# The gathers of the next expert's tokens moved from steps 11 to 14 of an expert to steps 9 to 12

## The chip, the cores and the metric

The kernel runs on one core of a Trainium2 chip. A core has a matrix engine (TensorE, PE in the profile; PEld are its weight loads, which overlap its products), a vector engine (VectorE, DVE), a scalar engine (ScalarE, ACT), GpSimd (POOL) and a queue engine (SyncE, SP) that here issues the loads of weights from HBM. The metric is the device time in microseconds (us) of one execution; lower is better.

## The reference

Two two-layer blocks run one after the other on 256 tokens of width 1024, all in float32. The change touches one part of the first block, the mixture of experts in its second layer:

```
def moe_swiglu(h, w_router, w_gate, w_up, w_down):
    logits = jnp.einsum('bsd,de->bse', h, w_router).astype(jnp.float32)
    top_v, top_i = lax.top_k(logits, TOP_K)
    wts = jax.nn.softmax(top_v, axis=-1)
    gates = jnp.sum(jax.nn.one_hot(top_i, N_EXPERTS, dtype=jnp.float32) * wts[..., None], axis=-2)
    ...
        a = jnp.einsum('sd,edf->sef', hb, w_gate)
        u = jnp.einsum('sd,edf->sef', hb, w_up)
        act = jax.nn.silu(a) * u * gb[:, :, None]
        return jnp.einsum('sef,efd->sd', act, w_down)
```

## The kernel before, in words

**Tiling.** Each expert computes only the tokens routed to it, at most 128 of them in one pass; a second pass exists in the code and is jumped over when no expert has more. The 3584 hidden columns of an expert are cut into 14 steps of 256 (`MOE_STEPS`), so the stage has 8 x 14 = 112 steps. A step loads 3 MiB of weights (1 MiB each for the two halves of gate and up, and one for down) into a ring of 6 slots, `ring`.

**Rounding to two terms.** Every float32 weight is used as a high and a low part. ACT writes the high part of a slot to another buffer (L637), DVE leaves the low part in the slot (L645), and `product` (L136 to L138) makes three matrix products of each pair of operands. PE can begin with a slot only after DVE's L645 on it.

**A step on each engine.** PE: `gate_up` (24 products of 512 columns), `down` of the step before (12 products), `turn` (two transposes, L2311). ACT: silu of the step (L2448), three high parts (L637), and a copy of the transposes (L2454). DVE: the product with silu's output (L2509), the low part of the transposes (L2513), three low parts (L645). SP waits until PE has finished `gate_up` or `down` on a slot, and then issues the next load into it, in the fixed order gate and up, gate and up, down (`moe_pass_sp`).

**The gather.** The tokens of the next expert are picked by products with a one-hot matrix: `gather(e1, g, ...)` in PE (L2290), for two of the eight chunks of 128 features, g = 0 to 3. Of each round ACT makes the high part (L2432) and DVE the low part (L2497, L2501); DVE's L2501 raises the semaphore `hTb`. Four such rounds fill `hTe`/`hLe` of the other half, a double buffer that alternates between experts. `gather` stands between `down` and `turn` of its step. Each round but the first waits for `hTb` of the round before, since all use the same piece of PSUM (`later_gather`). Ahead of the first product of the next expert, PE waits for the last `hTb`:

```
        pe.wait_ge(E['hTb'], e * 4 + (8 + moe_before(p, 'hTb')))
        gate_up(1 - half, 0, m1)
        down(1, m0 + (MOE_STEPS - 1), False, True)
        turn(m1)
        gate_up(1 - half, 1, m0 + (MOE_STEPS + 1))
        scatter(e)
```

The scatter (L2330) adds the finished expert's rows to the sum, in the second step of the next expert.

**Loops.** The program is written out by hand. An outer loop (L2240) runs three times over a pair of experts; experts 7 and 8 are written out behind it. In an expert an inner loop (L2336 in PE, L2252 in ACT and DVE) runs over pairs of steps up to `GATHER_STEP`, and the steps from there on are written out one by one, with the gathers. The first two steps of the next expert are written out as well. In the names of the trace `rT` is the one-hot matrix, `z_rounded` the high part of the gathered tokens, and `AT`, `AT_rounded` in one half and `ada`, `ada_rounded` in the other are the low part. Transposes of step n are called turn n here, counted from 1 to 14 in each expert.

Of the kernel before, what the change touches and what calls it, by code (L numbers as in the profile page):

```python
# [132 lines left out]
def product(pe, out, a, b, start, stop):  # L133


    pe.matmul(out, r32(a[0]), r32(b[1]), start=start, stop=False, skip_group_check=True)  # L136
    pe.matmul(out, r32(a[1]), r32(b[0]), start=False, stop=False, skip_group_check=True)  # L137
    return pe.matmul(out, r32(a[0]), r32(b[0]), start=False, stop=stop, skip_group_check=True)  # L138
# [18 lines left out]
def chunks(ap, k, w):  # L157

    return ap[:, 0:k * w].rearrange('p (k w) -> p k w', k=k)
# [469 lines left out]
def ffn_slot(st, q, r):  # L629
    return (st['j0'] + 3 * r + q) % RING  # L630
# [1495 lines left out]
MOE_STEPS = F_EXPERT // FT  # L2126
# [24 lines left out]
def moe_sems(c, p):  # L2151

    E = {name: c.s[name if p == 0 else f'again_{name}'] for name in ('gu_hi', 'gu_lo', 'down_hi', 'down_lo')}
    return E | {name: c.s[f'me_{name}'] for name in MOE_COUNTS}


def moe_before(p, name):
    return p * MOE_COUNTS[name]
# [72 lines left out]
def moe_split_value(st, q, m, p):  # L2231
    return split_value(st if p == 0 else dict(split0=0), q, m)


GATHER_STEP = MOE_STEPS - 4


def moe_experts(eng, expert):

    with eng.Fori(0, (N_EXP - 2) // 2) as pair:  # L2240
        for half in range(2):
            expert(pair * 2 + half, pair * (2 * MOE_STEPS) + half * MOE_STEPS, half, None)
    for e in (N_EXP - 2, N_EXP - 1):
        expert(e, e * MOE_STEPS, e % 2, e)


def moe_body_loop(eng, body, extra, next_extra, end):


    def expert(e, m0, half, known):  # L2250
        last = known == N_EXP - 1
        with eng.Fori(1, GATHER_STEP // 2) as it:  # L2252
            for r in range(2):
                body(r, m0 + it * 2 + r, 2, None)
        for i in range(GATHER_STEP, MOE_STEPS):
            ahead = min(2, MOE_STEPS - 1 - i) if last else 2
            body(i % 2, m0 + i, ahead, None if last else (lambda i=i: extra(e, half, i - GATHER_STEP)))
        if last:
            end(e)
            return  # L2260
        body(0, m0 + MOE_STEPS, 2, lambda: next_extra(e, known))
        body(1, m0 + (MOE_STEPS + 1), 2, None)
    for r in range(2):
        body(r, r, 2, None)
    moe_experts(eng, expert)


def first_gather(c, g):

    return c.pb[4 + g][:, 0:S]  # L2270


def later_gather(c):
    return c.pb[7][:, S:2 * S]


def moe_pass_pe(c, pe, st, p):
    E = moe_sems(c, p)
    G, T = c.pb[6], c.pb[7]

    def gather(e1, g, out, before):

        if g == 0:
            pe.wait_ge(E['onehot'], e1 + moe_before(p, 'onehot'))
        elif before is not None:
            pe.wait_ge(E['hTb'], before)
        for i in range(2):
            kc = 2 * g + i
            for n in range(NT):
                mm = pe.matmul(out[:, i * P:i * P + P], c.xn[:, n, kc * P:kc * P + P], c.onehot[:, n, :],  # L2290
                               start=n == 0, stop=n == NT - 1)
        mm.then_inc(E['gathered'], 1)

    def parts(q, r, n):
        slot = ffn_slot(st, q, r)
        return chunks(c.hi_moe[slot], n, SLOT // n), chunks(c.ring[:, slot, :], n, SLOT // n)

    def gate_up(half, r, m):
        hTe, hLe = c.hTe[half], c.hLe[half]
        for q in range(2):  # L2300
            pe.wait_ge(E['gu_lo'], moe_split_value(st, q, m, p))
            wh, wl = parts(q, r, 4)
            for i in range(4):
                x = 4 * q + i
                mm = product(pe, G[:, :], (hTe[:, x, :], hLe[:, x, :]), (wh[:, i, :], wl[:, i, :]), x == 0, x == KD - 1)
        mm.then_inc(E['gu'], 1)

    def turn(m):
        pe.wait_ge(E['act'], m + (1 + moe_before(p, 'act')))
        for a in range(2):  # L2310
            mm = pe.transpose(T[:, a * P:a * P + P], c.fa[:, 0, a * P:a * P + P], c.ident[:, :])  # L2311
        mm.then_inc(E['turned'], 1)

    def down(r, m, first, last):
        pe.wait_ge(E['down_lo'], moe_split_value(st, 2, m, p))
        pe.wait_ge(E['actT'], m + (1 + moe_before(p, 'actT')))
        wh, wl = parts(2, r, 2)
        for h in range(2):
            col = slice(h * 512, h * 512 + 512)
            for a in range(2):  # L2320
                mm = product(pe, c.pb[4 + h][:, :], (c.faT[:, 0, a, :], c.faL[:, 0, a, :]), (wh[:, a, col], wl[:, a, col]),
                             first and a == 0, last and a == 1)
        mm.then_inc(E['down'], 1)

    def scatter(e):
        pe.wait_ge(E['ye'], e + (1 + moe_before(p, 'ye')))
        pe.wait_ge(E['sums'], e + (1 + moe_before(p, 'sums')))
        for n in range(NT):
            for h in range(2):
                mm = pe.matmul(c.pb[2 * n + h][:, :], c.combine[:, n * P:n * P + P], c.ye[:, h * 512:h * 512 + 512],  # L2330
                               start=False, stop=False, skip_group_check=True)
        mm.then_inc(E['scat'], 1)

    def expert(e, m0, half, known):
        last = known == N_EXP - 1
        with pe.Fori(1, GATHER_STEP // 2) as it:  # L2336
            for r in range(2):
                m = m0 + it * 2 + r
                gate_up(half, r, m)
                down(1 - r, m - 1, False, False)  # L2340
                turn(m)
        for i in range(GATHER_STEP, MOE_STEPS):
            g = i - GATHER_STEP
            gate_up(half, i % 2, m0 + i)
            down(1 - i % 2, m0 + (i - 1), False, False)
            if not last:
                gather(e + 2, g, later_gather(c), e * 4 + (4 + g + moe_before(p, 'hTb')))
            turn(m0 + i)
        if last:
            down(1, m0 + (MOE_STEPS - 1), False, True)  # L2350
            scatter(e)
            return

        m1 = m0 + MOE_STEPS
# [6 lines that stand above are left out]
        down(0, m1, True, False)  # L2361
        turn(m0 + (MOE_STEPS + 1))
    for g in range(4):
        gather(1, g, first_gather(c, g), None)
    pe.wait_ge(E['hTb'], 4 + moe_before(p, 'hTb'))
    gate_up(0, 0, 0)
    turn(0)
    gate_up(0, 1, 1)
    down(0, 0, True, False)
    turn(1)  # L2370
    moe_experts(pe, expert)


# [577 lines left out]
```

## Time and profile before

| | us |
|---|---|
| median of 3 runs | 2813.42 (2812.7 to 2815.88) |
| the profiled execution | 2820.07 |
| its span, from the first to the last instruction | 2817.7 |
| PE busy | 2357.3 (84% of the span) |
| DVE busy | 1868.7 (66%) |
| ACT busy | 1333.8 (47%) |
| steps of the expert stage, first turn to last turn | 811.5 to 1854.4 |
| mean granted TensorE clock | 0.898 of full speed |

Shares are averages over stages with different limits; the expert stage takes about 1050 us of the span. A step of that stage is measured here from turn to turn, the starts of two L2311 rows of PE.

### The profile page before, as it was taken

How to read it: one execution, taken by the hardware profiler on the slowest of the kernel's cores; microseconds unless marked ns; L12 is line 12 of the kernel's file. 1: busy time of each engine (PE TensorE's matmuls, PEld its weight loads, DVE VectorE, ACT ScalarE, POOL GpSimd, SP SyncE). 2: the span in 40 equal slices, each digit the busy share in tenths (PEclk: the TensorE clock that was granted, in tenths of full speed). 3: DMA queues.
4: the chain of work that ended last, by engine and by line, in shares of the span. 5: the costliest groups of instructions: out<-in, count | busy, mean ns of one | idle time of the engine just before them, and what ended most of it. 6: DMA issues, size and time to landing. Idle time of an engine off the chain costs nothing.

```text
span 2817.7 us, 30853 instructions
## 1 busy us (share of the span) xinstructions
PE 2357.3 (84%) x11193; PEld 1935.7 (69%) x11193; DVE 1868.7 (66%) x1975; ACT 1333.8 (47%) x1416; POOL 42.2 (1%) x102
## 2 busy tenths in 40 slices
PE   4836899855689999999999999966869987476998
PEld 4726687744567787777777777846758876465786
DVE  7776766776468787878888887855444443544553
ACT  3412433522247676766776676742334443232542
POOL 1000000000000000000000000000000000000000
PEclk9856999976689999999999999977979998688999
DMA  8730687530159899999999998953315552131453
GB/s 304 259 108 15 212 294 279 189 105 0 45 172 357 304 354 314 353 314 336 334 334 340 323 344 306 359 201 120 124 44 181 191 176 87 60 105 59 136 179 127
DMA packets 412832, 594.81 MB, mean 211 GB/s; under 512 B 20315, under 2 KB 326726, under 8 KB 412742
## 3 DMA queue, kind: packets, MB, share of 16 engines
q1 hardware_dynamic: 407040, 586.55, 60.4%
q10 hardware_dynamic: 5702, 7.04, 0.7%
q8 instruction: 58, 0.95, 0.1%
q14 instruction: 32, 0.26, 0.0%
HBM read 592.47 MB, written 1.05 MB: 211 GB/s over the span
## 4 chain that ended last, share of the span: by engine, by line
PE 72%; DVE 13%; ACT 5%; issue 3%; DMA 3%; POOL 1%; SPq 0%; ACTq 0%; DVEq 0%; POOLq 0%
PE bank L136 21%; PE bank L138 20%; PE bank L137 20%; DMA ring<-in_moe_w_up 2%; DVE ring_rounded L645 1%; PE bank L2330 1%; PE bank L1135 1%; PE bank L1113 1%; DVE ring_rounded L287 1%; ACT L L1187 1%; PE bank L2290 1%; PE bank L2311 1%; PE bank L1651 1%; PE bank L1124 1%; PE bank L461 1%
## 5 line engine op out<-in xcount | busy, mean ns | idle before, releaser
L136 PE MATMUL bank<-ring_rounded,hT_rounded 128*128 128x512 f32 (+3 forms) x944 | 376.9, 399 | 50.2 <-DVE ring_rounded L287 47.4
L136 PE MATMUL bank<-ring_rounded,z_rounded 128*128 128x512 f32 x896 | 365.9, 408 | 24.9 <-DVE AT_rounded L2501 11.4
L645 DVE TENSOR_TENSOR ring_rounded<-ring,zT_rounded 128x2048 fp32r<-128x2048 f32 x147 | 336.9, 2292 | 62.9 <-ACT zT_rounded L637 61.1
L136 PE MATMUL bank<-ring_rounded,L_rounded 128*128 128x512 f32 x712 | 290.5, 408 | 15.8 <-DVE score_rounded L778 10.5
L637 ACT ACTIVATE zT_rounded<-ring 128x2048 fp32r<-128x2048 f32 x147 | 281.6, 1916 | 31.6 <-DMA ring<-in_moe_w_up 16.6
L136 PEld LDWEIGHTS bank<-ring_rounded,hT_rounded 128*128 128x128 f32 x944 | 183.0, 194 | 88.3 <-issue 54.4
L136 PEld LDWEIGHTS bank<-ring_rounded,z_rounded 128*128 128x128 f32 x896 | 170.6, 190 | 67.6 <-issue 21.5
L645 DVE TENSOR_TENSOR ring_rounded<-ring,PT_rounded 128x2048 fp32r<-128x2048 f32 x74 | 169.4, 2289 | 39.9 <-ACT PT_rounded L637 39.5
L645 DVE TENSOR_TENSOR ring_rounded<-ring,mix_rounded 128x2048 fp32r<-128x2048 f32 x71 | 162.5, 2288 | 29.3 <-ACT mix_rounded L637 29.0
L136 PEld LDWEIGHTS bank<-ring_rounded,L_rounded 128*128 128x128 f32 x712 | 134.3, 189 | 56.2 <-DVE ring_rounded L645 19.4
L637 ACT ACTIVATE PT_rounded<-ring 128x2048 fp32r<-128x2048 f32 x74 | 141.7, 1915 | 37.9 <-DMA ring<-in_moe_w_up 36.4
L637 ACT ACTIVATE mix_rounded<-ring 128x2048 fp32r<-128x2048 f32 x71 | 136.2, 1919 | 29.0 <-DMA ring<-in_moe_w_up 27.9
L645 DVE TENSOR_TENSOR ring_rounded<-ring,hT_rounded 128x2048 fp32r<-128x2048 f32 x56 | 128.3, 2291 | 27.1 <-ACT hT_rounded L637 27.1
L138 PE MATMUL bank<-zT_rounded,L_rounded 128*128 128x512 f32 x368 | 146.1, 397 | 0.0
L137 PE MATMUL bank<-zT_rounded,score_rounded 128*128 128x512 f32 x368 | 144.6, 393 | 0.0
L645 DVE TENSOR_TENSOR ring_rounded<-ring,hL_rounded 128x2048 fp32r<-128x2048 f32 x56 | 128.3, 2291 | 13.4 <-ACT hL_rounded L637 12.8
L745 ACT ACTIVATE L_rounded<-bank 128x256 fp32r<-128x256 f32 x66 | 25.3, 383 | 220.6 <-PE bank L696 220.5
L778 DVE TENSOR_TENSOR score_rounded<-bank,L_rounded 128x256 fp32r<-128x256 f32 x66 | 27.8, 421 | 146.1 <-ACT L_rounded L745 146.0
L137 PE MATMUL bank<-hT_rounded,ring_rounded 128*128 128x256 f32 x416 | 120.4, 290 | 0.0
L637 ACT ACTIVATE hT_rounded<-ring 128x2048 fp32r<-128x2048 f32 x56 | 107.3, 1916 | 24.4 <-DMA ring<-in_moe_w_up 24.1
L137 PE MATMUL bank<-PT_rounded,hL_rounded 128*128 128x512 f32 (+2 forms) x282 | 112.7, 400 | 0.0
L278 ACT ACTIVATE PT_rounded<-ring 128x2048 fp32r<-128x2048 f32 (+3 forms) x31 | 53.3, 1719 | 123.2 <-DVEq L2850 40.5
(464 smaller groups left out, 5547.4 us busy)
## 6 DMA issues: line engine op xcount, KB each, us to landing
ring<-in_moe_w_gate SPq DMA_DIRECT2D x224, 512.0 KB, 5.3
ring<-in_moe_w_up SPq DMA_DIRECT2D x224, 512.0 KB, 6.8
ring<-in_moe_w_down SPq DMA_DIRECT2D x224, 512.0 KB, 7.8
ring<-in_ffn_w_gate_up SPq DMA_DIRECT2D x88, 512.0 KB, 5.1
ring<-in_ffn_w_down SPq DMA_DIRECT2D x66, 512.0 KB, 7.9
ring<-in_w_ada SPq DMA_DIRECT2D x48, 512.0 KB, 7.1
ring<-in_w_in SPq DMA_DIRECT2D x32, 512.0 KB, 4.9
xn<-in_w_ada SPq DMA_DIRECT2D x24, 512.0 KB, 9.6
```

The lines of the kernel that those rows point to most:

```text
L136: pe.matmul(out, r32(a[0]), r32(b[1]), start=start, stop=False, skip_group_check=True)
L137: pe.matmul(out, r32(a[1]), r32(b[0]), start=False, stop=False, skip_group_check=True)
L138: return pe.matmul(out, r32(a[0]), r32(b[0]), start=False, stop=stop, skip_group_check=True)
L278: act.activation(r32(st['hi'][(s - st['s0']) % H][:, 0:n]), c.ring[:, j % RING, 0:n], ACT.Copy)\
L287: dve.tensor_tensor(r32(words), words, high(st['hi'][(s - st['s0']) % len(st['hi'])][:, 0:n]), ALU.subtract)\
L461: mm = pe.transpose(c.pb[j][:, i * S + n * P:i * S + n * P + P], c.xn[:, n, kc * P:kc * P + P], c.ident[:, :])
L637: act.activation(r32(hi[slot]), c.ring[:, slot, :], ACT.Copy).then_inc(sem, 1)
L645: dve.tensor_tensor(r32(w), w, high(hi[slot]), ALU.subtract).then_inc(sem_out, 1)
L1113: mm = pe.matmul(c.pb[bank][:, u * S:u * S + s], a['q'](i, n), a['k'](i, n), start=True, stop=True)
L1124: mm = pe.transpose(c.pb[4 + b % 3][:, (blk % 4) * P:(blk % 4) * P + P], c.L[:, i * S + ch * P:i * S + ch * P + P], c.ident[:, :])
L1135: mm = pe.matmul(out, v, c.PT[:, blk * P:(blk + m) * P], start=x == 0, stop=x == len(terms) - 1)
L1187: act.activation(row, row, ACT.Exp, bias=c.nmx[:, i:i + 1], scale=a['scale'], accum_out=c.esum[:, i:i + 1]).then_inc(c.s['att_exp'], 1)
```

## The change

The four gathers stand in steps 9 to 12 of an expert (its last two steps have none), where they stood in steps 11 to 14. For that, the inner loop ends two steps earlier, and six steps are written out in place of four.

```
-GATHER_STEP = MOE_STEPS - 4
+GATHER_STEP = MOE_STEPS - 6
+GATHERS = 4
...
         for i in range(GATHER_STEP, MOE_STEPS):
             ahead = min(2, MOE_STEPS - 1 - i) if last else 2
-            body(i % 2, m0 + i, ahead, None if last else (lambda i=i: extra(e, half, i - GATHER_STEP)))
+            g = i - GATHER_STEP
+            body(i % 2, m0 + i, ahead, None if last or g >= GATHERS else (lambda g=g: extra(e, half, g)))
...
             gate_up(half, i % 2, m0 + i)
             down(1 - i % 2, m0 + (i - 1), False, False)
-            if not last:
+            if not last and g < GATHERS:
                 gather(e + 2, g, later_gather(c), e * 4 + (4 + g + moe_before(p, 'hTb')))
             turn(m0 + i)
```

Line numbers below the changed places are higher by 2 in the new kernel (L2311 is L2313 there).

PE before, end of the first expert of a pair (last products of `down`, last gather, turn 14, then the wait and the next expert's first `gate_up`):

```order
L137 MATMUL bank<-hL_rounded,score_rounded 128x512
L138 MATMUL bank<-hL_rounded,L_rounded 128x512
L2286 REGISTER_ALU
L2290 MATMUL bank<-rT,xn 128x128 x4
L2309 REGISTER_ALU
L2311 MATMUL bank<-ident,L 128x128 x2
L2355 REGISTER_ALU
L2301 ISA
L136 MATMUL bank<-ring_rounded,z_rounded 128x512
```

PE in the changed kernel, the same place:

```order
L137 MATMUL bank<-hL_rounded,score_rounded 128x512
L138 MATMUL bank<-hL_rounded,L_rounded 128x512
L2311 REGISTER_ALU
L2313 MATMUL bank<-ident,L 128x128 x2
L2357 REGISTER_ALU
L2303 ISA
L136 MATMUL bank<-ring_rounded,z_rounded 128x512
```

The gather's four products are gone from here; two whole steps now lie between the last of them and this place.

DVE before, step 14 of the first expert of a pair (low part of a slot, of the transposes, of the gathered tokens, then two slots):

```order
L645 TENSOR_TENSOR ring_rounded<-ring,hT_rounded 128x2048
L2513 TENSOR_TENSOR score_rounded<-bank,L_rounded 128x256
L2493 REGISTER_ALU
L2497 TENSOR_SCALAR ada<-bank,modA,modC 128x128 x2
L2501 TENSOR_TENSOR ada_rounded<-ada,z_rounded 128x256
L643 REGISTER_ALU
L645 TENSOR_TENSOR ring_rounded<-ring,zT_rounded 128x2048
L643 ISA
L645 TENSOR_TENSOR ring_rounded<-ring,PT_rounded 128x2048
```

DVE in the changed kernel, step 14:

```order
L645 TENSOR_TENSOR ring_rounded<-ring,hT_rounded 128x2048
L2515 TENSOR_TENSOR score_rounded<-bank,L_rounded 128x256
L643 REGISTER_ALU
L645 TENSOR_TENSOR ring_rounded<-ring,zT_rounded 128x2048
L643 ISA
L645 TENSOR_TENSOR ring_rounded<-ring,PT_rounded 128x2048
```

The three operations of the gather left step 14 (and step 13) and stand in the same place of steps 9 and 10.

## Rows read from the trace of the kernel before

**Rows 1.** The page: span, busy time, and 40 slices of the span.

```profile
span 2817.7 us, 30853 instructions
...
PE   4836899855689999999999999966869987476998
...
PEclk9856999976689999999999999977979998688999
DMA  8730687530159899999999998953315552131453
```

**Rows 2.** Waits of PE and SP, 929 to 1739 us: total, times, longest.

```profile
PE bank L136 <- DVE ada_rounded L2501: 11.4, 4, 2.9
PE bank L136 <- DVE AT_rounded L2501: 8.6, 3, 2.9
...
PE bank L136 <- DVE ring_rounded L645: 1.1, 2, 0.6
...
PEld bank L136 <- DVE ring_rounded L645: 8.5, 25, 1.0
```

**Rows 3.** Timeline from a turn 14 to the next expert's products: start, us, engine.

```profile
1195.41 0.38 PE L2311 MATMUL bank<-ident,L 128*128 128x128 f32 x2
...
1195.91 0.81 ACT L2432 ACTIVATE z_rounded<-bank,modC,modA 128x128 fp32r<-128x128 f32 x2 [1.96 <-PE bank L2311]
...
1197.03 0.42 DVE L2513 TENSOR_TENSOR score_rounded<-bank,L_rounded 128x256 fp32r<-128x256 f32 x1 [0.72 <-ACT L_rounded L2454]
1197.37 0.72 DVE L2497 TENSOR_SCALAR ada<-bank,modA,modC 128x128 f32<-128x128 f32 x2
1198.12 0.42 DVE L2501 TENSOR_TENSOR ada_rounded<-ada,z_rounded 128x256 fp32r<-128x256 f32 x1
...
1198.68 0.49 PE L136 MATMUL bank<-ring_rounded,z_rounded 128*128 128x512 f32 x1 [2.88 <-DVE ada_rounded L2501]
1199.01 0.40 PE L137 MATMUL bank<-mix_rounded,ada_rounded 128*128 128x512 f32 x1
...
1201.10 0.63 PE L137 MATMUL bank<-mix_rounded,ada_rounded 128*128 128x512 f32 x1
```

**Rows 4.** Windows, turn 14 to turn 1: us, engines' busy time, PEclk, DMA share, GB/s.

```profile
1195.41:1208.68 13.27, 10.39 (x41) 8.11 (x40) 7.67 (x9) 6.87 (x7) 0.00 (x0) 0.87 0.61 207
...
1460.18:1471.92 11.74, 8.86 (x40) 6.96 (x39) 7.94 (x9) 6.87 (x7) 0.00 (x0) 1.00 0.68 235
...
sum 91.15, PE 71.13 PEld 55.60 DVE 54.50 ACT 48.07 POOL 0.00; mean PE 10.16 PEld 7.94 DVE 7.79 ACT 6.87 POOL 0.00
```

**Rows 5.** Windows, turn 2 to turn 10 of seven experts, eight steps each.

```profile
1353.75:1422.05 68.30, 68.30 (x306) 55.47 (x305) 57.89 (x39) 51.01 (x40) 0.00 (x0) 1.00 1.01 349
...
sum 486.90, PE 483.65 PEld 386.35 DVE 407.91 ACT 358.42 POOL 0.00; mean PE 69.09 PEld 55.19 DVE 58.27 ACT 51.20 POOL 0.00
```

**Rows 6.** Windows, turn 10 to turn 14 of seven experts, four steps each.

```profile
1290.26:1328.57 38.31, 38.31 (x185) 31.27 (x185) 34.57 (x30) 27.30 (x27) 0.00 (x0) 1.00 0.99 339
...
sum 267.88, PE 267.26 PEld 218.86 DVE 240.88 ACT 191.37 POOL 0.00; mean PE 38.18 PEld 31.27 DVE 34.41 ACT 27.34 POOL 0.00
```

**Rows 7.** Window, turn 1 to turn 2, with the scatter.

```profile
1605.21:1617.12 11.91, 11.91 (x47) 8.45 (x46) 9.80 (x9) 7.26 (x7) 0.00 (x0) 1.00 1.04 358
```

**Rows 8.** DMA queues in the first pass of the outer loop, 829 to 1095 us.

```profile
q8 instruction: 6, 0.10, 0.2%
```

**Rows 9.** DMA queues from 1100 to 1600 us: all packets, and the one queue.

```profile
DMA packets 128130, 168.42 MB, mean 337 GB/s; under 512 B 5149, under 2 KB 114306, under 8 KB 128130
...
q1 hardware_dynamic: 128130, 168.42, 97.5%
```

**Rows 10.** Branches of PE's sequencer, and PE behind the second: ns min/median/max, starts.

```profile
L2240 PEldq COMPARE_BRANCH  x3: 67/209/217, 1084.9 to 1613.9; - x3
...
L2215 PEldq COMPARE_BRANCH  x1: 4832/4832/4832, 1866.9 to 1866.9; - x1
...
1871.81 1.10 PE L2420 MATMUL bank<-zero 128*128 128x256 f32 x2 [2.07 <-issue]
```

## The prediction

> **What bounds the kernel now.** I read the page's slices first. From about slice 12 to slice 27, the expert stage, PE is at nine tenths or more and its clock is full but for a dip here and there; the DMA engines are as busy [rows 1]. So two resources are near their limit there, and the question is which one PE waits for. The waits of PE over six experts answer it: there is one large entry, DVE's L2501, in seven waits of 2.9 us each, 11.4 + 8.6 = 20.0 us in all; on weights (DVE's L645) PE itself waits 1.1 us in total, and its weight loads 8.5 us in 25 small pieces [rows 2]. L2501 is the last low part of the gathered tokens, and seven is the number of passages from one expert to the next.
>
> The timeline of one passage shows the chain [rows 3]. Turn 14 starts at 1195.41. ACT can take the last gather only when turn 14 is done (L2432 at 1195.91, released by L2311), because its gather stands behind its wait for the turn; DVE follows with L2513, L2497 and L2501, which ends at 1198.54; PE starts the next expert's first product at 1198.68. PE's own idle time is 2.88 us. Behind it the record of a product grows from 0.40 us to 0.63, so the passage costs more than the idle time.
>
> The windows price it whole. From turn 14 to turn 1 of the next expert takes 13.27 us with a mean granted clock of 0.87; in one passage of the seven the clock stayed at 1.00, and it took 11.74 [rows 4]. Thus the drop of the clock from its upper level (2.4 GHz) to its lower (1.2 GHz) for a few us behind the idle stretch is worth 1.5 us, six times. The seven passages together are 91.15 us [rows 4]. A step with neither gather nor scatter, averaged over 56 of them, takes 486.90 / 56 = 8.69 us, and in the best expert 68.30 / 8 = 8.54 [rows 5]. A step with a gather takes 267.88 / 28 = 9.57 us, with PE busy in 267.26 of the 267.88 us [rows 6]: the gather there is PE's own work, 0.88 us more. The step with the scatter takes about 11.9 us [rows 7].
>
> **The change part by part.**
>
> *The gathers on PE.* The same four rounds, 0.88 us each, move from the steps that end in turns 11 to 14 to those that end in turns 9 to 12. Removed and added work cancel: 0. No wait is added. The first round needs the one-hot matrix, written by DVE in the first step of the same expert, eight steps earlier; each further round needs L2501 of the round before, as now, with a step between them. The buffer that they fill was last read by the expert before. No DMA is issued by them. SP waits for the ends of `gate_up` and `down`, whose order is unchanged.
>
> *ACT and DVE.* They get the same operations two steps earlier. In a step with a gather DVE is busy 240.88 / 28 = 8.60 us of 9.57 [rows 6], in one without it 407.91 / 56 = 7.28 of 8.69 [rows 5]. Both fit, and the new steps 13 and 14 are of the second kind.
>
> *The wait for `hTb`.* It is satisfied two steps, some 17 us, before PE comes to it. The passage then is a step like any other: `gate_up`, `down`, turn. What is late next is a slot of weights, since the first `gate_up` of the next expert needs L645 on its slots. In the timeline of now that low part was made a step ahead, as in all other steps, so I take the average plain step, which has such waits in it. 91.15 - 7 x 8.69 = 91.15 - 60.8 = **30.3 us** gained, of which 20.0 is idle time and the rest mostly the clock. With the plain step of the best expert it would be 91.15 - 7 x 8.54 = 31.4.
>
> *The loads.* Where I charge nothing for them, the cover is this. A step loads 3 x 1.049 = 3.146 MB. The stall now gives the DMA a rest: 207 GB/s in that window [rows 4]. Without it an expert takes 9 x 8.69 + 4 x 9.57 + 11.9 = 128.4 us for 44.0 MB, 343 GB/s on average; the windows show 349 over eight steps and 358 in the step of the scatter, when the queue catches up [rows 5, 7]. At 358 GB/s a step's load takes 8.79 us: 0.78 less than a step with a gather and 0.1 more than a plain one. The four gather steps let the loads run up to the limit of the ring, and the three plain steps that now lie between them and the scatter (steps 13, 14 and the next expert's first) give back 0.3. The scatter's 3.3 us then refill the ring, as now, so what follows it starts from the same state. Up to 1 us per passage may still be lost, the longest single wait for weights [rows 2]; this goes into the range.
>
> *The code.* Six steps are written out in place of four, in each half of the outer loop's body. By the counts of the windows a step is 76 instructions on PE (305 products and as many weight loads in eight steps) [rows 5], a gather 16 more and the scatter about as many [rows 6, 7]: the body grows from 16 x 76 + 8 x 16 + 2 x 16 = 1376 to 20 x 76 + 160 = 1680. In its first pass PE's instruction queue fetched 6 blocks [rows 8]; in the 500 us after 1100, with two returns to the start of the body in sight of it, none at all: the only queue with packets is that of the loads [rows 9]. So the chip keeps the present body, and whether it keeps one of 1680 / 1376 x 6 = 7.3 blocks no row shows. Bounds: nothing, if it does; if it does not, a jump to code that is not there is the 4.83 us branch at L2215, behind which PE was idle 2.07 us [rows 10]. The jump back at L2240 is taken with a lead: the sequencer is there at 1613.9, turn 2 begins at 1617.12 [rows 7, 10], 3.2 us later. That leaves 4.8 - 3.2 = 1.6 us per jump, two jumps, 3.2 us. I take nothing, as the nearest row shows no fetch [rows 9], and keep 3.2 for the range.
>
> The Trainium skill, Runtime: NRT & Kernel Launch, section Instruction fetch mechanics, speaks against the change here: it gives PE a store of 128 KiB, 2048 instructions in blocks of 16 KiB, eight of them, and says that a taken branch whose target is outside a window of two blocks forces a fetch. By its two-block window the present kernel would fetch at each return, which the trace contradicts; by its 2048 instructions the new body, which would touch eight blocks and call for a ninth, is just at the limit. That page would give 3.2 us less gain, the row as it stands gives none.
>
> **The sum.** 30.3 us off the profiled execution's 2820.07 is 2789.8. That execution is 6.65 us over the median of the runs, 2813.42; carried over, 2783.1.
>
> **The rivals.**
>
> 1. *Refetch at the return.* The body no longer fits by one block: 2 x 1.6 = 3.2 us, 2786. For it: it grows by a fifth. Against: nothing in the trace but the lead of the sequencer, which hides most of it.
>
> 2. *Weights take the stall's place.* PE now comes to the next expert 4.3 us earlier each time, and the loads were almost continuous before. If the three plain steps ahead of the scatter each waited 0.5 us, half the longest wait seen, it is 7 x 3 x 0.5 = 10.5, so 2794. For it: DMA share 1.01 to 1.04 in the windows [rows 5, 7]. Against: PE lost only 486.90 - 483.65 = 3.3 us to idle time in 56 plain steps.
>
> 3. *DMA is the true bound.* If the loads could not do more than the 337 GB/s seen between 1100 and 1600 us [rows 9], an expert needs 130.7 us; now it takes 8 x 8.69 + 4 x 9.57 + 13.02 + 11.9 = 132.7, so 2.0 x 7 = 14 us, 2799; at the 332 that the present pace amounts to (44.0 MB in 132.7 us), nothing, 2813. Against: the 358 above.
>
> 4. *Slower: the code streams through.* If the store works so that a body one block too long misses in every block, two passes of eight blocks at up to 4.83 us are 77 us, of which sequential fetching hides some. It decides from 30.3 / 16 = 1.9 us exposed per block on; fully exposed it is 2783 + 77 = 2860. Against: in the first pass, where each block was new as well, PE showed no other waits than in the later ones [rows 2].
>
> **How the numbers follow.** A measurement of this kernel can tell about 0.2%, 5.6 us, from no change. Forecast 0.60; rival 1 0.15; rival 2 0.14; rival 3 0.06 (half of it within 0.2%); rival 4 0.03, and 0.02 that the passages stay as they are for a reason I don't see. Faster: 0.60 + 0.15 + 0.14 + 0.03 = 0.92. Same: 0.03 + 0.02 = 0.05. Slower: 0.03. The range reaches from 2779 (the best expert's plain step, 2782, less the spread of the runs, 3 us) to 2796 (rival 2 and the spread).
>
> **What would show it.** No wait of PE for L2501 at the seven passages; turn 14 to turn 1 at 8.5 to 8.8 us with a clock of 1.00; turn 8 to turn 12 at 9.57 a step; the DMA rate over the stage from 332 to 343 GB/s. Rival 1 shows as blocks on the instruction queue during the second and third pass and a gap behind L2240's successor; rival 2 as waits for L645 in steps 13 to 1. The forecast is wrong if those waits exceed 1 us a passage, or if a clock below 1.00 remains in the stage.

## The result and the profile after

| | before | changed |
|---|---|---|
| median of 13 runs, us | 2818.26 | 2799.32 |
| profiled execution, us | 2820.07 | 2796.46 |
| its span, us | 2817.7 | 2794.7 |

The ratio of the times is 0.9939, with a 95% interval of 0.9925 to 0.9954: 0.61% faster, 17 us, where 1.08% (30.3 us) was forecast. One run of 5986.56 us, more than twice the others, is left out of the ratio.

The waits of PE from 905 to 1730 us in the changed kernel (total, times, longest), to be held against [rows 2]:

```profile
PE bank L136 <- issue: 6.7, 2, 3.5
PE bank L136 <- DVE ring_rounded L645: 1.4, 2, 1.1
PE bank L2313 <- DVE L L2511: 0.5, 2, 0.3
```

The seven waits for the gathered tokens, 20.0 us, are gone. In their place stand two waits of 3.3 and 3.5 us that the profile ascribes to "issue": PE waited for nothing it shows. The windows of the passages, turn 14 to turn 1 (us, busy time of each engine, clock, DMA share, GB/s), answer to [rows 4]:

```profile
927.70:936.34 8.64, 8.64 (x39) 6.97 (x39) 7.48 (x5) 6.64 (x6) 0.00 (x0) 1.00 1.05 362
...
1316.59:1325.08 8.49, 8.49 (x40) 6.93 (x38) 7.24 (x5) 5.80 (x5) 0.00 (x0) 1.00 1.04 361
...
1704.93:1715.23 10.30, 9.01 (x40) 6.69 (x38) 7.54 (x5) 7.99 (x6) 0.00 (x0) 1.00 0.99 337
sum 62.69, PE 61.16 PEld 47.69 DVE 52.43 ACT 47.31 POOL 0.00; mean PE 8.74 PEld 6.81 DVE 7.49 ACT 6.76 POOL 0.00
```

91.15 us became 62.69, a gain of 28.5, and the clock stays at 1.00 in every one. The four steps with a gather, now turn 8 to turn 12, cost what they did in [rows 6]:

```profile
sum 266.71, PE 266.71 PEld 218.87 DVE 240.08 ACT 191.58 POOL 0.00; mean PE 38.10 PEld 31.27 DVE 34.30 ACT 27.37 POOL 0.00
```

What was given back stands at turn 2 to turn 3 of experts 3 and 5, right behind the outer loop's return; the same steps of the kernel before took 8.49 and 8.48 us by the same reading of its turns:

```profile
1076.65:1090.30 13.65, 10.38 (x40) 8.12 (x38) 5.71 (x5) 6.17 (x5) 0.00 (x0) 0.87 0.47 150
1337.15:1350.79 13.64, 10.19 (x39) 8.02 (x38) 5.72 (x5) 6.17 (x5) 0.00 (x0) 0.87 0.49 157
```

27.3 - 17.0 = 10.3 us. PE's own timeline of the first of them (start, us, what, idle time before) shows both parts of the 5.2 us, the idle stretch and then records of 0.63 us at a lower clock:

```profile
1076.65 0.38 PE L2313 MATMUL bank<-ident,L 128*128 128x128 f32 x2
1080.31 0.49 PE L136 MATMUL bank<-ring_rounded,z_rounded 128*128 128x512 f32 x1 [3.27 <-issue]
...
1082.21 0.63 PE L136 MATMUL bank<-ring_rounded,z_rounded 128*128 128x512 f32 x1
...
1084.97 0.40 PE L137 MATMUL bank<-hT_rounded,AT_rounded 128*128 128x512 f32 x1
```

The instructions of the outer loop's line on PE's sequencer (ns least, median, most; first and last start), against [rows 10], and the DMA queues from 1100 to 1600 us, against [rows 9]:

```profile
L2241 PEldq COMPARE_BRANCH  x3: 74/6421/6457, 1073.4 to 1595.2; - x3
```

```profile
q1 hardware_dynamic: 130939, 171.23, 99.5%
q8 instruction: 15, 0.25, 0.2%
```

The branch that took 0.2 us takes 6.4 when it is taken (the third, which falls through, takes 0.07). Code is fetched all through the second and third pass: 15 packets of 16 KiB, one block of code each, in a stretch where there was none. Three numbers make the account of the span: 28.5 us gained at the passages, 10.3 lost at the two returns, and the rest of the 23.0 us, 4.8, which is spread. Of that rest 2.3 us lie ahead of the stage, whose first turn starts at 809.3 in place of 811.5, 1.2 in the steps with a gather, and the remainder in small differences of the other steps.

### The profile page after: what moved, and what is told of

The parts are those of the page before. It is cut to its first block, busy times and chain, and to the rows that moved or that the text cites. A ratio compares the mean times of both kernels' runs of the same rounds, so it can differ in the third digit from the quotient of the medians.

```text
span 2794.7 us, 30741 instructions
## 1 busy us (share of the span) xinstructions
PE 2351.6 (84%) x11193; PEld 1931.9 (69%) x11193; DVE 1868.2 (67%) x1975; ACT 1334.5 (48%) x1416; POOL 42.0 (2%) x102
## 4 chain that ended last, share of the span: by engine, by line
PE 71%; DVE 10%; ACT 5%; DMA 3%; issue 3%; POOL 1%; SPq 0%; ACTq 0%; DVEq 0%; POOLq 0%
PE bank L136 21%; PE bank L138 20%; PE bank L137 20%; DMA ring<-in_moe_w_up 2%; DVE ring_rounded L645 1%; PE bank L2332 1%; PE bank L2313 1%; PE bank L2292 1%; PE bank L1651 1%; PE bank L1113 1%; PE bank L1135 1%; ACT L L1187 1%; DVE ring_rounded L287 1%; PE bank L461 1%; ACT PT_rounded L278 1%
## 5 line engine op out<-in xcount | busy, mean ns | idle before, releaser
L645 DVE TENSOR_TENSOR ring_rounded<-ring,zT_rounded 128x2048 fp32r<-128x2048 f32 x147 | 336.9, 2292 | 53.3 <-ACT zT_rounded L637 51.7
L645 DVE TENSOR_TENSOR ring_rounded<-ring,PT_rounded 128x2048 fp32r<-128x2048 f32 x74 | 169.4, 2290 | 38.2 <-ACT PT_rounded L637 37.8
L645 DVE TENSOR_TENSOR ring_rounded<-ring,mix_rounded 128x2048 fp32r<-128x2048 f32 x71 | 162.5, 2289 | 31.3 <-ACT mix_rounded L637 31.1
L645 DVE TENSOR_TENSOR ring_rounded<-ring,hT_rounded 128x2048 fp32r<-128x2048 f32 x56 | 128.3, 2292 | 33.0 <-ACT hT_rounded L637 33.0
L645 DVE TENSOR_TENSOR ring_rounded<-ring,hL_rounded 128x2048 fp32r<-128x2048 f32 x56 | 128.3, 2292 | 12.4 <-ACT hL_rounded L637 11.2
```

Of the source, the lines that this page charges most:

```text
L645: dve.tensor_tensor(r32(w), w, high(hi[slot]), ALU.subtract).then_inc(sem_out, 1)
```

## The experiments

Two theories of the loss. **Code**: the outer loop's body no longer stays with PE, and each return waits for its first block to be fetched (this is rival 1 of the prediction, at a higher price). **Loads**: PE reaches the weights earlier than they come, and the long branch only shows where. Each run is compared with the kernel before on the same chip. The first four ran on one chip and the last three on another, so a difference between two runs of different chips is a difference of two ratios, and a tenth of a per cent in it says little.

**The layout alone.** Six steps are written out as in the change, but the gathers stay in steps 11 to 14, in PE and in the other engines.

```
-            g = i - GATHER_STEP
+            g = i - (MOE_STEPS - GATHERS)
...
-            if not last and g < GATHERS:
+            if not last and g >= 0:
```

> The code of the change with the gathers back in steps 11 to 14: six steps written out in each half, as in the changed kernel. Theory (the outer loop's body no longer stays with PE and is fetched again at each of its two returns, 5.1 us of step time each): the seven passages cost 13.2 us each as before, and the two returns add 10 us; 10 us slower than the kernel before, 0.36%, with branches of 6.4 us at the outer loop's end. Rival (the long branches have to do with the gathers' new place or with the weights arriving later): no long branch here, same time as before.

0.58% slower (ratio 1.0058, 1.0045 to 1.0070), 16 us. The branch, the two steps behind it, and the instruction queue from 1100 to 1600 us:

```profile
L2241 PEldq COMPARE_BRANCH  x3: 74/6477/7701, 1083.2 to 1626.0; - x3
```

```profile
1086.45:1098.49 12.04, 8.73 (x40) 6.96 (x38) 5.97 (x6) 6.17 (x5) 0.00 (x0) 1.00 0.54 174
1356.13:1371.02 14.89, 10.33 (x39) 8.11 (x38) 5.71 (x5) 6.17 (x5) 0.00 (x0) 0.89 0.42 145
```

```profile
q8 instruction: 15, 0.25, 0.2%
```

The gathers are where they were, the passages cost 91.8 us as before, and the two returns 26.9 - 17.0 = 9.9 us more. So the loss belongs to the code layout, not to the new place of the gathers. In the first of the two steps the clock held (1.00), and the step is shorter by about what that is worth. The total is 6 us more than the theory gave. Three steps with a gather that took 10.3 to 10.5 in place of 9.6 us, each with a wait of 0.6 us for L645, are 2.5 of it; the kernel before has one such step.

**The change in one half.** Only experts 1, 3, 5 and 7 gather early, so that the body has 18 steps.

```
+def gather_step(half):
+    return MOE_STEPS - (4 if half else 6)
...
-        with pe.Fori(1, GATHER_STEP // 2) as it:
+        with pe.Fori(1, gather_step(half) // 2) as it:
```

> The change in the first half of the pair alone: experts 1, 3, 5 and 7 gather in steps 9 to 12 with six steps written out, experts 2, 4 and 6 stay as before. The outer body has 18 steps in place of 16 (before) and 20 (changed). Theory (a limit between 16 and 20 steps, about 8 blocks of code): four passages fall from 13.2 to about 9.0 us, 4 x 4.1 = 16.5 us faster than before; if 18 steps still fit, no long branch and that is all, 0.59% faster; if the limit is below 18, 10 us less, 0.23%. Rival (any longer body is fetched again): the second number.

0.64% faster (0.9936, 0.9924 to 0.9947). The four early passages together, and the branch:

```profile
sum 34.25, PE 34.25 PEld 27.67 DVE 29.86 ACT 25.32 POOL 0.00; mean PE 8.56 PEld 6.92 DVE 7.47 ACT 6.33 POOL 0.00
```

```profile
L2244 PEldq COMPARE_BRANCH  x3: 67/209/217, 1082.8 to 1601.3; - x3
```

8.56 us a passage and no long branch, and no packet on the instruction queue from 1100 to 1600 us. Half the change is worth as much as the whole, since a body of 18 steps still stays.

**PE's outer loop written out.** All eight experts stand one behind the other in PE's program; the other engines keep their loops. Once with the change, once with the kernel before as a control.

```
-    moe_experts(pe, expert)
+    for e in range(N_EXP):
+        expert(e, e * MOE_STEPS, e % 2, e)
```

> The changed kernel with PE's outer loop over pairs of experts written out (all eight experts one after the other; the inner loops over steps stay; the other engines keep their loops). Theory: PE never jumps back to code that has left, the two steps of 13.65 us become 8.56, and it is 10.2 us faster than the changed kernel, 28 to 30 us or 1.0% faster than before. Rival (the loss is a wait for weights or for DMA, which the branch only shows): the two steps stay long, no gain.

> The kernel before with PE's outer loop written out, as a control. Theory: its body was not fetched again anyway, and the seven passages stay at 13.2 us; within 2 us of the kernel before. Rival (written out code is faster or slower by itself): a difference of more than 5 us.

With the change 0.97% faster (0.9903, 0.9890 to 0.9916), 0.36% or 10 us better than the ratio of the changed kernel. The control is 0.12% faster (0.9988, 0.9977 to 1.0000), 3 us, where within 2 us was expected; so up to some 3 of the 10 us may come from writing the loop out as such. The two steps themselves, 13.65 and 13.64 us in the changed kernel, are 8.49 and 8.48 although PE comes to them no later than in the changed kernel and needs the same weights, which speaks against the theory of the loads. But not all passages are short now:

```profile
1177.70:1187.27 9.57, 8.99 (x40) 6.72 (x38) 7.54 (x5) 7.39 (x6) 0.00 (x0) 1.00 0.98 339
...
1564.01:1574.75 10.74, 9.21 (x39) 6.64 (x37) 7.54 (x5) 7.11 (x6) 0.00 (x0) 1.00 1.03 355
1692.79:1702.28 9.49, 8.79 (x39) 6.86 (x39) 7.52 (x5) 6.33 (x6) 0.00 (x0) 1.00 1.06 363
...
1328.66:1337.14 8.48, 8.48 (x39) 6.93 (x38) 5.62 (x5) 6.18 (x5) 0.00 (x0) 1.00 0.72 249
```

**The same body, shifted.** In the run with one half, new blocks were asked for at 837, 899, 921, 948, 1030 and 1055 us, and the next one only at 1607, right behind the loop (packets of the instruction queue in the trace). PE was thus near the end of a block at each return. 25 products of zeros over 8 columns, ahead of the stage, move the same 18 steps about 100 instructions on (the trace has 50 weight loads and 50 products of that line). They add zeros to a bank of the output. The kernel before with the same 25 products is the control.

```
+    for _ in range(25):
+        pe.matmul(c.pb[0][:, 0:8], c.zero[:, 0:P], c.zero[:, 0:8], start=False, stop=False, skip_group_check=True)
     for g in range(4):
         gather(1, g, first_gather(c, g), None)
```

> The kernel of e2_one_half with 25 small products of zeros (8 columns, added to a bank of the output, so that nothing changes in it) ahead of the stage, about 100 instructions: the outer body is the same 18 steps, but starts about 100 instructions later in its block of 256. In e2_one_half the last new block was asked for at 1055 us and the next only behind the loop, so PE was near the end of its seventh block at each return. Theory (eight blocks are held, one of them the block asked for ahead; a body that enters an eighth block loses the first): long branches of 6.4 us at both returns, 10 us slower than e2_one_half beside the 3 to 5 us of the products themselves; 0.15 to 0.25% faster than before. Rival (the limit is on the number of instructions in the body, or the refetch has to do with the changed steps): as e2_one_half but for the products, 0.45 to 0.5% faster than before.

> Control for the run above: the kernel before with the same 25 small products ahead of the stage. Its body of 16 steps, shifted as well, still ends ahead of an eighth block. Theory: no long branch, and only the price of the products, 3 to 5 us, 0.1 to 0.2% slower than before. Rival (any shift of the code costs fetches at the returns): 13 us slower.

The control is 0.21% slower (1.0021, 1.0007 to 1.0036), the price of the products. Its branch stays short, and its instruction queue has no packet from 1100 to 1600 us:

```profile
L2240 PEldq COMPARE_BRANCH  x3: 78/221/221, 1089.0 to 1616.1; - x3
```

The shifted half is 0.55% slower than before (1.0055, 1.0035 to 1.0075), where 0.15 to 0.25% faster was expected, and about 1.2% slower than the same body unshifted. Branch, the steps behind it, and PE's two idle stretches in the first of them:

```profile
L2244 PEldq COMPARE_BRANCH  x3: 74/6341/6517, 1089.9 to 1628.9; - x3
```

```profile
1093.12:1111.10 17.98, 10.78 (x40) 8.32 (x39) 6.20 (x6) 6.17 (x5) 0.00 (x0) 0.81 0.36 120
1362.78:1380.32 17.54, 11.16 (x39) 8.59 (x38) 5.71 (x5) 6.17 (x5) 0.00 (x0) 0.81 0.36 119
```

```profile
1096.85 0.49 PE L136 MATMUL bank<-ring_rounded,z_rounded 128*128 128x512 f32 x1 [3.35 <-issue]
...
1101.19 0.59 PE L137 MATMUL bank<-mix_rounded,AT_rounded 128*128 128x512 f32 x1 [3.85 <-issue]
```

That the loop's body is fetched again when it is only shifted is the theory's; the size is not. I had one stall per return, and there are two. The target now lies close to the end of its block, and the next block, gone as well, is needed before it has come: PE makes one product and stops, the packet of the second block leaves at 1098.9 us, and PE goes on 2.3 us later. At the second return it is the same (idle for 3.3 and 3.1 us, going on 2.4 us behind the second packet). 35.5 - 17.0 = 18.5 us are lost at the returns, 5 in the products, and 5 to 6 more elsewhere in the stage.

**The gathers first.** Gathers in steps 3 to 6, written out, and the inner loop behind them, in ACT and DVE as in PE (only PE's part is shown): no gather is left near a passage, and the body has 16 steps as before.

```
-GATHER_STEP = MOE_STEPS - 6
+GATHER_STEP = 2
...
+        for g in range(GATHERS):
+            i = GATHER_STEP + g
+            gate_up(half, i % 2, m0 + i)
+            down(1 - i % 2, m0 + (i - 1), False, False)
+            if not last:
+                gather(e + 2, g, later_gather(c), e * 4 + (4 + g + moe_before(p, 'hTb')))
+            turn(m0 + i)
+        with pe.Fori((GATHER_STEP + GATHERS) // 2, MOE_STEPS // 2) as it:
```

> The gathers in steps 3 to 6 of an expert, written out, and the inner loop behind them over steps 7 to 14. The outer body has 16 steps again, as before, and eight steps lie between the last gather and the wait. Theory (what the change gains at the passages is real, what it loses is the fetching of its longer body): no long branch, the instruction queue idle in the second and third pass, all seven passages at 8.5 to 9 us; 29 to 33 us faster than before, 1.0 to 1.15%, and 10 us faster than the changed kernel. Rival (nine plain steps in a row outrun the loads, so that waits for weights take 1 us or more an expert): under 24 us, 0.85%.

1.06% faster than before (0.9894, 0.9874 to 0.9914): medians 2785.7 against 2815.6, 29.9 us. The seven passages, the branch, and the queues from 1100 to 1560 us:

```profile
sum 60.10, PE 60.10 PEld 48.55 DVE 52.54 ACT 45.38 POOL 0.00; mean PE 8.59 PEld 6.94 DVE 7.51 ACT 6.48 POOL 0.00
```

```profile
L2241 PEldq COMPARE_BRANCH  x3: 67/209/225, 1076.0 to 1588.0; - x3
```

```profile
q1 hardware_dynamic: 120996, 158.67, 99.6%
```

No long branch, no code fetched in the later passes, PE busy through every passage. It is the change without its side effect. Its ratio is the lowest of the study, though the intervals do not tell it from the changed kernel with PE's loop written out (0.9894 and 0.9903).

## Why the prediction was wrong

**What bounds the kernel: right.** The wait for `hTb` was on the path, and it was worth the idle time and the clock behind it: 91.15 us became 62.69 in the changed kernel and 60.10 in the best one.

**The gathers on PE, ACT and DVE: right.** 267.88 us for the 28 steps before, 266.71 after.

**The passages: right in kind, a little small in size.** Forecast 8.69 us each; measured 8.96, of which two passages with waits for weights are most of the excess (9.09 and 10.30). Without code being fetched it is 8.56 (one half) and 8.59 (gathers first). The term of 30.3 us measured 28.5, and up to 31.0.

**The loads: right in the main.** The rate the windows showed did carry the faster pace: the passages run at 358 to 369 GB/s but for the last (337), which has the one wait for L645 of more than 1 us. From 1100 to 1600 us the mean is 343 GB/s. Rival 2 did not come beyond that passage. Rival 3 did not either: its time, 2799, is the one measured, but by chance, since its condition was that the rate stays at 337, and the kernel with the gathers first, with a mean of 345, is faster by another 13 us.

**The code: this is the step that failed.** "I take nothing, as the nearest row shows no fetch" was the choice, with 3.2 us as the other bound. Measured: 10.3 us. So rival 1 is what happened, at three times its price, and both halves of the step were wrong. Whether: the body did not stay, at 20 steps. The 7.3 blocks of the prediction were scaled from the 6 fetched [rows 8]; but six fetches within the pass, each on entering a block, mean that the present body touches seven blocks and has an eighth asked for, so it was closer to a limit than the sum made it look. How much: the priced branch was 4.83 us, the real one is 6.4; taking off the lead of 3.2 us, PE is idle for 3.3 and 3.5, not 1.6; and the clock falls behind the idle stretch, 1.5 us more, which I had just read in [rows 3, 4] and did not carry over to this rival. 3.3 + 3.5 + 2 x 1.5 = 9.8 of the 10.3 us. One of the prediction's own signs of being wrong, a clock below 1.00 in the stage, came in just there (0.87 at both returns).

With 5.2 a return in place of nothing, the gain would have been 30.3 - 10.3 = 20.0 us, and the sum 2793. The ratio measured corresponds to a gain of 17 us, and the profiled pair of executions to 23.6. Of the 13 us between 30.3 and 17, the returns are thus 10.3 and the passages 1.8. The time forecast was besides 4.8 us too low from the start: it was carried over to a median of three runs, 2813.42, which became 2818.26 over thirteen.

**Rival 4** (each block missed, slower) did happen in its first half: the later passes fetch every block again. But PE is seen to wait only for the block at the return and, in the shifted half, for the next one; the others come in time. The changed kernel was not slower for it, since the passages gained more; the layout alone shows the sign that rival 4 feared, 0.58% slower.

## What to carry to other kernels

Writing steps out of a loop to move work is also a change of code size: count the instructions of the longest loop that returns, add the block asked for ahead, and look at the instruction queue in the second pass before pricing the rest. A price read at one place (a branch under light load, an idle stretch at the full clock) is to be carried with what follows it, here the clock. And when work must move earlier, moving it to the front of the loop body can leave the size as it was, where moving it by two steps did not.

## What the runs showed of the hardware

PE kept a body that touched seven blocks of code while an eighth had been asked for ahead: before, one half, gathers first and the shifted control have six packets on the instruction queue within the first pass and none in the later ones. A body that entered its eighth block, so that a ninth was asked for, has seven packets in the first pass and nine in the second: everything was fetched again (changed kernel, layout alone, and the shifted half with the same 18 steps). The Trainium skill, Runtime: NRT & Kernel Launch, section Instruction fetch mechanics, gives PE 2048 instructions in blocks of 256, which is eight; these runs agree. Its rule that a taken branch to a target outside a window of two blocks forces a fetch is not borne out: in the kernel before a return over six blocks took 0.2 us and fetched nothing.

A return to a block that had left took 6.3 to 6.5 us, once 7.7, with the loads running; the jump out of the stage took 4.6 to 5.5. The packets of the instruction queue show where the difference lies. Once the block's packet had left, the branch was over in 2.4 to 2.7 us in every case. But the packet left 3.7 to 3.9 us behind the branch's start at the returns (5.2 in the one of 7.7) and 2.1 to 3.0 at the jump. What holds the packet back was not tried.

Behind an idle stretch of PE of 2.7 to 3.5 us, once 4.6, the clock fell to the lower level for a while in most cases, and in some it did not, for the same code. It fell in six of seven passages before, in five of seven in the control with the outer loop written out, in three of seven in the shifted control, in all seven of the layout alone, but in only one of that kernel's two returns; over all nine traces in 24 of 34 passages with this stall. Where it held at 1.00, the step was about 1.5 us shorter.

What stays open: fetching code seems to cost a little besides the returns. In the kernels that fetch code all through the stage, single steps take about 1 us more with waits for L645 or L2512 (10.29, 10.50 and 10.44 in the layout alone, 9.57, 10.74 and 9.49 above). Over all nine traces there are seven steps with a gather that took 10.2 us or more. In six of them (three in the layout alone, one each in the kernel before and in the two with PE's loop written out) the wait stands 10.9 to 11.9 us behind a packet of the instruction queue; in the kernel before, that is the first packet after more than 600 us without one. The seventh, in the first steps of the stage with the gathers first, is not near a packet. Most packets are followed by no such wait, and no run changes the fetches alone, so this is a coincidence in time and no shown cause.
